# A hybrid encoder trunk on one core: last sample chunk's residual turned earlier for the router, and normed rows of chunks 5 to 9 turned through DRAM

## The reference, cut to what matters

```python
h = rmsnorm(x, mix_norm)                    # x * rsqrt(mean(x*x) + eps) * gain
... = split(h @ w_in)                       # 2848 columns: attention, SSD and mLSTM inputs
x = x + concat(window_attention, bidirectional_ssd, bidirectional_mlstm) @ w_out
x = x + expert_choice_ffn(rmsnorm(x, ffn_norm), router, w_gate, w_up, w_down)
```

## Time and profile before

| | us |
|---|---|
| median of 3 runs | 2242.45 (2242.13 to 2244.83) |
| the profiled execution | 2246.58 |
| its span, first to last instruction | 2245.1 |
| TensorE busy | 2219.8 |
| VectorE busy | 1235.4 |
| ScalarE busy | 617.7 |
| POOL busy | 564.9 |

### The profile page before, as it was taken

One profiled execution on the slowest core, in us unless ns is written; L12 is line 12 of the kernel. 1 busy time (PEld: TensorE's weight loads), 2 busy tenths in 40 slices (PEclk: granted clock), 3 DMA queues, 4 the chain that ended last, 5 costly groups with the idle time before them and its releaser, 6 DMA issues.

```text
span 2245.1 us, 32479 instructions
## 1 busy us (share of the span) xinstructions
PE 2219.8 (99%) x12464; PEld 1581.4 (70%) x12464; DVE 1235.4 (55%) x2404; ACT 617.7 (28%) x1421; POOL 564.9 (25%) x660
## 2 busy tenths in 40 slices
PE   9999999999999999999999999999999999999998
PEld 7557578874446888877775575888744468877786
DVE  3555466586765445554236554665867654555442
ACT  4221233474332111111132212334743311111111
POOL 1104455154311111111111044541442111111111
PEclk9999999999999999999999999999999999999999
DMA  4002122633657988888440021335346579878883
GB/s 160 21 20 76 57 94 94 164 115 126 211 182 269 339 294 292 278 275 290 141 131 21 21 75 56 99 107 134 113 145 203 191 277 351 281 272 299 291 290 74
DMA packets 179540, 388.84 MB, mean 173 GB/s; under 512 B 12181, under 2 KB 63897, under 8 KB 179386
## 3 DMA queue, kind: packets, MB, share of 16 engines
q1 hardware_dynamic: 162042, 344.68, 44.5%
q0 software_dynamic: 15264, 41.95, 7.6%
q10 hardware_dynamic: 2080, 0.13, 0.1%
HBM read 329.77 MB, written 56.96 MB: 172 GB/s over the span
## 4 chain that ended last, share of the span: by engine, by line
PE 89%; DVE 4%; ACT 2%; DMA 2%; issue 1%; POOL 0%; SPq 0%; DVEq 0%; ACTq 0%; POOLq 0%
PE ps L1989 87%; DVE TMP L1799 1%; DMA MID<-w_up 1%; PE ps L2015 1%; ACT SCR L1138 1%; DMA HT<-h_sample,idxs 1%; DVE SCR L1804 1%; DVE TMP L1804 0%; PE ps L2048 0%; DMA MID<-x_sample 0%; DVE HT L1360 0%; DVE HT L1931 0%; DVE TMP L1360 0%; ACT RING L1138 0%; DMA HT<-h_prompt,idxg 0%
## 5 line engine op out<-in xcount | busy, mean ns | idle before, releaser
L1989 PE MATMUL ps<-MID,HT 128*128 128x512 f32 (+3 forms) x2560 | 679.8, 490 | 1.8 <-DVE HT L1360 1.2
L1989 PEld LDWEIGHTS ps<-HT,MID 128*128 128x128 f32 x4096 | 555.4, 191 | 16.7 <-issue 15.0
L1989 PE MATMUL ps<-HT,MID 128*128 128x160 f32 (+1 forms) x4096 | 558.8, 298 | 1.2 <-DVE HT L1360 0.9
L1989 PEld LDWEIGHTS ps<-MID,HT 128*128 128x128 f32 (+1 forms) x2560 | 298.6, 156 | 284.9 <-issue 246.7
L1989 PE MATMUL ps<-RING,HT 128*128 128x256 f32 (+2 forms) x1760 | 387.3, 389 | 0.0
L1989 PEld LDWEIGHTS ps<-RING,HT 128*128 128x128 f32 (+1 forms) x1760 | 313.0, 190 | 59.9 <-issue 17.4
L1989 PE MATMUL ps<-HT,RING 128*128 128x512 f32 (+1 forms) x960 | 349.8, 522 | 0.0
L1989 PEld LDWEIGHTS ps<-HT,RING 128*128 128x128 f32 x960 | 180.2, 190 | 153.3 <-issue 145.2
L1931 DVE STREAM_TRANSPOSE HT<-HT 32x256 f32<-32x256 f32 x576 | 251.1, 436 | 18.4
L1369 DVE SCALAR_TENSOR_TENSOR HT<-HT,ps 128x160 f32<-128x160 f32 (+1 forms) x128 | 40.8, 319 | 396.9 <-ACT HT L1322 394.9
L932 POOL DMA_INDIRECT y_prompt<-SCR,idxp x32 | 50.3, 1573 | 584.0 <-ACT SCR L1332 543.2
(11 more groups left out here) (287 smaller groups left out, 2113.0 us busy)
## 6 DMA issues: line engine op xcount, KB each, us to landing
MID<-w_gate SPq DMA_DIRECT2D x32, 2048.0 KB, 8.9
MID<-w_up SPq DMA_DIRECT2D x32, 2048.0 KB, 14.8
MID<-w_down SPq DMA_DIRECT2D x32, 2048.0 KB, 15.3
RING<-w_in SPq DMA_DIRECT2D x20, 1024.0 KB, 5.3
SCR<-cs_rows SPq DMA_DIRECT2D x20, 1024.0 KB, 5.1
p_rows<-SCR SPq DMA_DIRECT2D x12, 768.0 KB
HT<-p_rows SPq DMA_DIRECT2D x48, 192.0 KB, 3.5
y_sample<-RING SPq DMA_DIRECT2D x16, 512.0 KB, 4.3
```

The source lines that it names most:

```text
L1989: return pe.matmul(out, a, b, start=start, stop=stop)
```

## The change

Two parts, in both layers.

The head: chunks 5 to 9 (XB = 5) are no longer turned by TensorE. VectorE multiplies the loaded rows by their root and by the gain (weigh_x), with the columns of each 32-wide block put together, into one of three buffers XP; SP stores them to a new DRAM tensor and loads them back in four blocks into XN[c]; VectorE's 32 by 32 transposes (turn_x on VectorE) write hT. For that the gain must lie along the columns on all partitions: TensorE's spread_gains makes it with eight matmuls into PSUM banks 3 and 4, and ScalarE copies it to GAINS. The ring slices 1 and 2 are issued after the blocks of chunk 8 and of chunk 9. ScalarE's order of squares and evacuations is changed. Three buffers, semaphores that count several things (par_loaded, cst_loaded, softplus_exp, scratch_stored) and the counts waited for change with it.

The router: in the step of the first prompt chunk (n = 8), TensorE's order is changed so that turn_h2 of the last sample chunk comes right behind the logits of the chunk before; its logits go to PSUM bank 2; VectorE and ScalarE copy the turned residual before they treat the chunk before; one output projection matmul fewer stands ahead of the affinities.

The diff, with the other uses of the new counts left out:

```diff
+XB = 5
+X_STORED = 16 * (NC - XB)
+
+
+def ht_at(c):
+
+    return 2 * c + 2 if c < XB else XB + c + 1
...
+        xnr = nc.dram_tensor("x_norm_rows", ((NC - XB) * P, D), F32, kind="Internal").ap()
...
+        GAINS = TMP[:, 0:D]
+        XP = [Z[:, 0:4, 256:512], Z[:, 4:8, 256:512], XSF[:, 3328:4352].rearrange("p (b w) -> p b w", b=4)]
...
                     for c in range(NP, NC):
                         x_load(c)
-                    ring_load(1)
+
+                    def x_store(c):
+                        sp.wait_ge(scaled_odd, 2 + c - XB + 1)
+                        sp.dma_start(xnr[(c - XB) * P:(c - XB + 1) * P, :].rearrange("t (b w) -> t b w", b=4), XP[c % 3]).then_inc(scratch_stored, 16)
+
+                    def x_blocks(c):
+                        if c >= XB + 2:
+                            sp.wait_ge(ht_copied, ht_at(c - 2))
+                        rows = xnr[(c - XB) * P:(c - XB + 1) * P, :]
+                        for b in range(4):
+                            sp.dma_start(XN[c][32 * b:32 * b + 32, :].rearrange("p (a w) -> p a w", a=4),
+                                         rows[:, 256 * b:256 * (b + 1)].rearrange("(a j) w -> j a w", a=4)).then_inc([par_loaded, cst_loaded][c % 2], 16)
+
+                    x_store(XB)
+                    for c in range(XB, NC):
+                        sp.wait_ge(scratch_stored, 16 * (c - XB + 1))
+                        if c + 1 < NC:
+                            x_store(c + 1)
+                        x_blocks(c)
+                        if c == NC - 2:
+                            ring_load(1)
                     ring_load(2)
...
-                    sp.wait_ge(scratch_stored, 48)
+                    sp.wait_ge(scratch_stored, X_STORED + 48)
...
                     square(0)
                     square(1)
-                    for c in range(2, NC):
+                    square(2)
+                    square(3)
+                    scale_x(2)
+                    act.wait_ge(ht_made, 5)
+                    link(act.copy(GAINS[:, 0:512], ps[:, 3, :]))
+                    link(act.copy(GAINS[:, 512:1024], ps[:, 4, :]), softplus_exp)
+                    square(4)
+                    square(5)
+                    evac(0)
+                    scale_x(4)
+                    for c in range(6, NC):
                         square(c)
-                        if c % 2 == 0:
-                            scale_x(c)
-                        if c >= 3:
-                            evac(c - 3)
+                        evac(c - 5)
+                    evac(NC - 5)
+                    evac(NC - 4)
                     for u in range(NC - 3, NC):
                         evac(u)
-                    act.wait_ge(par_loaded, 16 * (layer + 1))
+                    act.wait_ge(par_loaded, seen["par"])
...
                     def keep_h2(c, j):
-                        act.wait_ge(parts_folded, c)
+                        act.wait_ge(parts_made, c)
                         act.wait_ge(h2t_made, 2 * (c - LAST_SAMPLE) + j + 1)
...
-                        link(act.copy(LGP, ps[:, 3, 0:P]), parts_kept)
+                        link(act.copy(LGP, ps[:, 2 if c == LAST_SAMPLE else 3, 0:P]), parts_kept)
...
                     keep_logits(n - 2)
                     square_out(n - 1)
+                    keep_h2(n - 1, 1)
                     route_exp(n - 2)
-                    keep_h2(n - 1, 1)
                     keep_logits(n - 1)
+                    route_exp(n - 1)
                     keep_p(n + 1, 0, 1)
-                    route_exp(n - 1)
...
-                            dve.wait_ge(ht_made, 2 * c + j + 1)
+                            dve.wait_ge(ht_made, 2 * c + j + (1 if c < 2 else 2))
...
+                    def weigh_x(c):
+                        if c == XB:
+                            dve.wait_ge(softplus_exp, 1)
+                        dve.wait_ge(rooted, c + 1)
+                        if c >= XB + 3:
+                            dve.wait_ge(scratch_stored, 16 * (c - 2 - XB))
+                        x, g = XN[c].rearrange("p (k b i) -> p k b i", b=4, i=32), GAINS.rearrange("p (k b i) -> p k b i", b=4, i=32)
+                        for b in range(4):
+                            out = XP[c % 3][:, b, :].rearrange("p (k i) -> p k i", i=32)
+                            link(dve.scalar_tensor_tensor(out=out, in0=x[:, :, b, :], scalar=rs[:, c:c + 1], in1=g[:, :, b, :],
+                                                          op0=ALU.mult, op1=ALU.mult), scaled_odd if b == 3 else dve_chain, wait=b == 3)
+
+                    def turn_x(c):
+                        base = seen["blocks"][c % 2]
+                        dve.wait_ge([par_loaded, cst_loaded][c % 2], base + 64 * ((c - XB - (c - XB) % 2) // 2 + 1))
+                        link(dve.transpose(hT[:, :, c * P:(c + 1) * P].rearrange("p k (a j) -> p a k j", a=4),
+                                           XN[c].rearrange("p (a k i) -> p a k i", a=4, k=KD)), ht_copied)
+
                     keep_ht(0)
-                    for c in range(1, NC):
+                    for c in range(1, XB):
                         if c % 2 == 1:
                             scale_x(c)
                         keep_ht(c)
                         if c == 3:
+                            weigh_x(XB)
                             scale_first()
+                            weigh_x(XB + 1)
+                    weigh_x(XB + 2)
+                    for c in range(XB, NC):
+                        turn_x(c)
+                        if c + 3 < NC:
+                            weigh_x(c + 3)
...
                     def keep_h2(c):
-                        dve.wait_ge(parts_folded, c)
+                        dve.wait_ge(parts_made, c)
...
                     add_x(n - 1, 1)
                     keep_y(n + 1, 0)
+                    keep_h2(n - 1)
                     route_shift(n - 2)
-                    keep_h2(n - 1)
...
                             if c >= 2:
                                 pe.wait_ge(ht_copied, 2 * c - 3 + j)
+                            if c == 2 and j == 0:
+                                pe.wait_ge(softplus_exp, 1)
...
-                            pe.wait_ge(ht_copied, 2 * g + (1 if k1 <= KD // 2 else 2))
+                            pe.wait_ge(ht_copied, ht_at(g) - (1 if k1 <= KD // 2 else 0))
...
+                    def spread_gains():
+                        pe.wait_ge(par_loaded, seen["par"])
+                        for k in range(KD):
+                            last = mm(ps[:, 3 + k // 4, k % 4 * P:(k % 4 + 1) * P], pr("gmix")[:, k:k + 1].to_broadcast([P, P]), ident)
+                        last.then_inc(ht_made, 1)
+
                     turn_x(0)
                     if layer == 0:
                         run_idle(3)
...
                     pe.wait_ge(rooted, 1)
                     mm(ps[:, 2, 0:P], rs[:, 0:1].to_broadcast([P, P]), ident).then_inc(rs_spread, 1)
                     turn_x(1)
+                    spread_gains()
                     if layer > 0:
                         unit(1)
-                    for c in range(2, NC):
+                    for c in range(2, XB):
                         turn_x(c)
                         if c > 2 or layer == 0:
                             unit(c - 1)
-                    unit(NC - 1)
+                    for c in range(XB - 1, NC):
+                        unit(c)
...
-                        if 1 <= c <= LAST_SAMPLE:
+                        if 1 <= c < LAST_SAMPLE:
                             pe.wait_ge(lg_shift, c)
+                        if c == LAST_SAMPLE:
+                            pe.wait_ge(yt_copied, 3 * (NC - 1))
+                        bank = 2 if c == LAST_SAMPLE else 3
                         rows = rout2 if c < LAST_SAMPLE else part[:, ROUTER:ROUTER + (KD + 1) * E]
                         for k in range(KD):
                             j = k % 4
-                            last = mm(ps[32 * j:32 * j + 32, 3, 0:P], rows[:, k * E:(k + 2) * E], H2T[:, k, :], k < 4, k >= 4)
+                            last = mm(ps[32 * j:32 * j + 32, bank, 0:P], rows[:, k * E:(k + 2) * E], H2T[:, k, :], k < 4, k >= 4)
                         last.then_inc(parts_made, 1)
 
                     def fold_logits(c):
                         pe.wait_ge(parts_kept, c + 1)
+                        if c == LAST_SAMPLE:
+                            pe.wait_ge(lg_shift, c)
                         mm(ps[:, 6 if c == NC - 2 else 3, 0:E], LGP, FOLD[:, 0:E]).then_inc(parts_folded, 1)
...
                     n = NC - 2
-                    out_proj(n, 0, 0, 1)
                     logits(n - 2)
-                    out_proj(n, 0, 1, 2)
-                    fold_logits(n - 2)
                     turn_h2(n - 1, 0)
                     turn_h2(n - 1, 1)
-                    out_proj(n, 0, 2, 3)
+                    out_proj(n, 0, 0, 1)
+                    fold_logits(n - 2)
                     logits(n - 1)
```

(14 more changed lines are left out.)

10 lines of the change are left out of this document (5 added, 5 removed).

## The result

The changed kernel took 2251.12 us (median of 9 runs, 2245.43 to 2255.09) against 2242.22 us before (2240.89 to 2244.83): a ratio of 1.0035, 95% interval 1.0027 to 1.0044. It is slower, by 8.9 us, where 6.45 us less was forecast, and it lies above the whole range of 2232.5 to 2240.8. The profiled execution took 2254.15 us, its span 2252.7; it lies 3.0 above its median, as that of before lies 4.1 above its own.

What follows compares the result with a forecast made beforehand. TensorE, busy 99% of the span, was taken as the bound. Heads 2.05 and 4.0, less 0.8 for the trip, plus 1.2 for the router, gave 6.45 us: median 2236.0 from 2242.45, range 2232.5 to 2240.8.

Steps and rivals of the forecast that it cites:

- blocks(9) wait only for the store and the turn of 7, are in at 50.6 against 52.4: Head of layer 0: chunk 9's block loads, held only by store and chunk 7's turn, land at 50.6, wanted by 52.4.
- order in the queue: Head, SP's queue: blocks move only once slice 1 is in; chunk 9 at 55.0, 4.4 us lost, 2240.4; chance 0.17.
- The trip: Head: store and load of chunks 5 to 9 through DRAM costs TensorE 0.8 us in layer 0, nothing in layer 1.
- The heads' own terms: Head, TensorE: dropped transposes less the gains' spread and waits save 2.05 us in layer 0, 4.0 in layer 1.
- the 4.0: Head of layer 1: 4.35 us of transposes saved, less 0.37 for turn_x(3) coming later.
- The router: Router, both layers: earlier transposes turn the affinities 0.6 us sooner and remove the 0.83 top-k wait; 1.2 us in all.
- The clock upwards: Head of layer 1: clock holds across the 1.9 us gap before turn_x(3), 1.7 us more won, 2235.2; chance 0.12.

Runs made afterwards that it cites:

- slices_last: The changed kernel with ring slice 1 issued behind the blocks of chunk 9, so both slices stand behind all blocks; 2241.22 us, ratio 0.9994.
- trip_early: Kernel with both slices behind all blocks, plus chunk 5's weighing ahead of chunk 3's eviction on VectorE and chunk 6's right behind it; 2237.78 us.
- weigh_ahead: Kernel of the early trip, with chunk 8's weighing ahead of chunk 5's turn and chunk 9's right behind that turn; 2235.78 us, ratio 0.9964.
- router_only: The kernel before with only the router's part of the change, the head of each layer as before; 2241.36 us, ratio 0.9998.
- router_scale3: The kernel before with the router's part and, in layer 1, chunk 3's scaling ahead of chunk 2's eviction on VectorE; 2240.93 us, ratio 0.9994.
- slice2_first: The changed kernel with slice 2 issued ahead of the first store, slice 1 left between the blocks of chunks 8 and 9; 2248.12 us, ratio 1.0029.
- slice1_first: The changed kernel with slice 1 issued ahead of the first store, slice 2 left behind the blocks of chunk 9; 2241.18 us, ratio 0.9994.
- wait_filled: The changed kernel with 18 (layer 0) and 10 (layer 1) unused matmuls keeping TensorE busy in the wait for chunk 9; 2251.54 us, ratio 1.0034.

## Why the prediction was wrong

**The step that failed** is "blocks(9) wait only for the store and the turn of 7, are in at 50.6 against 52.4". They waited for slice 1 too: in layer 0 the last of them landed at 57.7. In slices_last, where no slice stands ahead of them, it landed at 50.9, so the rest of that step was right. The prediction had this as a rival, order in the queue, and set it aside because "5.3 is mostly latency, which overlaps". The runs show the opposite: behind the slice the blocks take 6.5 us and more, instead of the 3.5 that they take in slices_last, and moving the slices gives back 9.9 us. The Trainium skill ("DMA: Bandwidth & Descriptors", section "Queues, rings and completion order"), cited there, says that on each DMA engine descriptors are consumed in ring order. The trace agrees as far as a slice ahead of the blocks goes; the 9.4 us of the last block, with a slice behind it, are not explained by it. The blocks did not wait for the whole slice: the first three landed at 52.9 to 54.3, the slice at 54.7. No run issued the slice from another engine's queue, so it stays open whether that would have spared them.

The 5.3 was itself too low for this place: it is the median of 20 slices of the whole run. In the head of before the same two slices, issued right behind the chunk loads, took more than three times that; so the trace of before already had loads that paid for what was issued ahead of them. Its DMA view, 0 to 60 us:

```profile
RING<-w_in SPq DMA_DIRECT2D x2, 1024.0 KB, 18.6
```

**The rival was right in kind and too small**: chunk 9 at 55.0 and 4.4 us lost for the two layers. The turn ended at 59.50. Slice 1 went out at 45.91, not 43.75; 0.9 of this is the issue of chunk 8's blocks, which took SyncE 2.61 us and not the 1.75 of the earlier trace rows, the rest came down the chain before it. From the slice's issue to the last block's landing it was 11.8 us instead of 10.0; the last block alone took 2.7 more than the one before it. Slice 2, right behind the blocks, was not counted; that the 2.7 are its doing is not shown. And the clock fell, which the rival left out: 7.14 and 5.81 us for a projection of 3.9 to 4.1.

**The trip** was second: 0.8 us lost in layer 0 and none in layer 1 was forecast. With the slices out of the way it was 0.93 + 0.71 + 0.18 = 1.82 and 0.92 + 0.52 + 1.64 = 3.08 us, and the first matmul after each wait adds a quarter of a microsecond (4.12 against 3.88). In layer 0 of slices_last the turn of chunk 5 ended at 36.89 against 36.25, mostly by the slower issue (2.57 us for the four blocks), and the turn of chunk 7 came 8.71 us behind it against 8.35. In layer 1, counted from the layer's first turn, the turn of chunk 5 ended 1.1 us later than forecast (31.36 against 30.21), and TensorE wanted it 1.0 sooner, since the clock held behind the wait of 1.93 us. The prediction had priced the next store and its weighing ahead of each group of blocks, but took their place as given: trip_early and weigh_ahead win 3.4 and 2.0 us by starting the weighings sooner.

**The heads' own terms** were right in layer 0: turn_x(2) at 18.03 against 17.9, the clock held across the 1.44 us wait, and five chunks lost their transposes as forecast. In layer 1 the 4.0 was taken off a profile whose head had lost more to the clock than others do: the unchanged head takes 55.01 us there and 53.47 in router_only. Against the latter slices_last gains nothing (53.57): the waits for the trip eat most of what the transposes give.

**The router** was right: 0.6 us forecast, 0.65 and 0.45 measured in the profile, and its wait gone in both layers. The medians of router_only do not show it.

**The clock upwards** came, but not shown to be by the matmuls that the rival named: unit 2 held, 4.05 us, and in router_only, which has no such matmuls ahead of the same wait, it held as well. It won nothing, since the first projection of that layer ran at half clock instead, 5.81 us.

The range adds up to 2232.6 and 2240.7 from the prediction's own numbers, 0.1 inside of what it states; nothing hangs on that.

## What to carry to other kernels

A load of 128 KB behind a megabyte on the same queue took 5.7 to 9.7 us here, and about 3.5 without it: put bulk loads that are needed later behind the small ones that are needed now, or well ahead of all. Take the price of a load from rows of the place where it will stand, not from the median of the run. When a chain is moved to DMA, follow it through the issuing queue one entry at a time, with what each entry waits for; here the weighings moved sooner were worth 5.4 us in two steps, and the chain without them nothing that could be told from before. And give a wait of TensorE of some microseconds a second price beside the wait, the half clock behind it: here 1.4 to 3.1 us for one projection behind waits of 2.02, 2.17, 2.93, 3.32 and 5.36 us, and none behind one of 2.52.

## What the runs showed that was not expected

**One wait, two clocks.** The first expert's transposes wait for the gathered rows 1.53 us before, 1.49 in router_only and 1.48 in router_scale3. In the first two the granted clock is 0.50 behind it until about 697; in the third it holds, and the stage behind takes 429.70 us instead of 432.0. TensorE's timeline of router_scale3, and under it that of router_only:

```profile
690.36 1.09 PE L2552 MATMUL ps<-cstt,HT 128*128 128x128 f32 x8 [1.48 <-DMA HT<-h_sample,idxs]
```

```profile
690.52 1.97 PE L2550 MATMUL ps<-cstt,HT 128*128 128x128 f32 x8 [1.49 <-DMA HT<-h_sample,idxs]
```

In the same way the wait of 2.52 us in slice2_first was followed by a full clock, that of 2.02 by half. In layer 1's head the wait of 1.93 us ahead of chunk 3's turn stands in ten of the kernels; the clock fell around it in three (before, slice1_first, wait_filled). The executions of one kernel differ in the same way: six of router_only took 2240.48 to 2241.36 us at a mean granted clock of 0.999, the other five 2243.03 to 2244.26 at 0.997.

The Trainium skill ("TensorE: Matmul & The Clock Gate", section "What's actually happening") says of the rise to the full clock that its point varies from run to run of one kernel. The rows here show falls, and they vary too.

So whether the clock falls behind a wait of 1.5 to 2.5 us could not be foretold here from the wait's length, and a fall is worth about 2 us; a sum made on one profiled execution carries it along. The profile of before had both this fall and two in the head of layer 1; they may well be most of the 4.1 us by which it stood above its median, which no run was made to show.

**The gather of layer 0 is shorter in every kernel with the trip**, by 0.7 to 1.1 us (table: 9.0 against 9.9; by 0.3 in wait_filled). In layer 1 it is not (8.4 to 8.7 with the trip, 8.68 before). No run isolates why; it stays open.
